# Router and experts of a three-part block: selection ahead of the list, and the residual kept in PSUM

## What is computed

```python
h2 = rms_norm_3(x, norm_ffn_w[l], NORM_EPS)
x = x + hierarchical_moe(h2, ...)
return rms_norm_3(x, final_norm_w, NORM_EPS)

def hierarchical_moe(h, w_gr, b_gr, w_er, b_er, w_gate, w_up, w_down):
    # each token picks one of 8 groups, and the best two of that group's 8 experts
    weights = g_gate[:, None] * jax.nn.softmax(top_v, axis=-1)
    ...
    def expert_block(args):
        xblk, e = args
        hid = jax.nn.silu(xblk @ w_gate[e]) * (xblk @ w_up[e])
        return hid @ w_down[e]
    ...
    out = jnp.zeros((n_tok, d)).at[buf_tok].add(yb * buf_w[:, None])
```

## Time and profile before

| | us |
|---|---|
| three runs: median (lowest to highest) | 2837.94 (2836.89 to 2840.13) |
| profiled execution, its own time | 2836.18 |
| its span in the trace | 2834.4 |
| TensorE busy (matmul), share of the span | 2708.1 (96%) |
| TensorE weight loads | 2280.6 (80%) |
| DVE busy | 1438.2 (51%) |
| ACT busy | 515.2 (18%) |
| DMA moved | 589.09 MB, 208 GB/s on average |

### The profile page before, as it was taken

How to read it: one execution, slowest core, us unless ns; L and a number is a source line. 1 busy time by engine, 2 the same in 40 slices (tenths; PEclk the granted TensorE clock), 3 DMA queues, 4 the chain that set the end, 5 groups by cost and what they waited for, 6 DMA issues and landing times. The chain is left out here.

```text
span 2834.4 us, 44443 instructions
## 1 busy us (share of the span) xinstructions
PE 2708.1 (96%) x18750; PEld 2280.6 (80%) x18750; DVE 1438.2 (51%) x2805; ACT 515.2 (18%) x1095; POOL 0.2 (0%) x4
## 2 busy tenths in 40 slices
PE   8999899999999999999999999999998898888887
PEld 8998799999988999888988998888896554444443
DVE  7768677687555775544345657365434111111112
ACT  1001410010043100223010012344302111111111
POOL 0000000000000000000000000000000000000000
PEclk9999999999999999999999999899999999999999
DMA  7644145355354453536544444555554899999997
GB/s 232 212 157 156 52 157 179 134 182 176 120 134 149 151 177 116 135 108 156 170 149 149 155 121 107 150 150 133 137 171 182 339 427 426 426 426 426 427 427 332
DMA packets 371212, 589.09 MB, mean 208 GB/s; under 512 B 17104, under 2 KB 328688, under 8 KB 348912
## 3 DMA queue, kind: packets, MB, share of 16 engines
q1 hardware_dynamic: 366256, 582.21, 58.4%
q10 hardware_dynamic: 4800, 4.63, 0.6%
HBM read 585.72 MB, written 1.08 MB: 207 GB/s over the span
## 5 line engine op out<-in xcount | busy, mean ns | idle before, releaser
L844 PE MATMUL bank<-hR,ring 128*128 128x128 f32 x2112 | 267.4, 277 | 3.9 <-DVE hR L426 3.9
L3498 DVE TENSOR_TENSOR wk<-bank,wk 128x256 f32<-128x256 f32 x43 | 26.1, 608 | 466.5 <-PE bank L3421 466.5
L844 PEld LDWEIGHTS bank<-hR,ring 128*128 128x128 f32 x2112 | 252.7, 194 | 4.9 <-DMA ring<-in_ffn_w_in 2.7
L3441 PE MATMUL bank<-ring,wk 128*64 128x512 f32 x688 | 157.1, 598 | 24.1 <-ACT wk L3458 24.1
L3421 PE MATMUL bank<-ring,wk 128*64 128x256 f32 x1344 | 153.0, 381 | 19.6 <-DMA ring<-in_w_expert_up 19.6
L3421 PEld LDWEIGHTS bank<-ring,wk 128*64 128x64 f32 x1344 | 94.3, 137 | 85.3 <-DMA ring<-in_w_expert_up 26.8
L1164 PE MATMUL bank<-big,ring 128*128 128x128 f32 x1320 | 159.6, 275 | 0.0
L1164 PEld LDWEIGHTS bank<-big,ring 128*128 128x128 f32 x1320 | 153.5, 192 | 0.1
L733 PE MATMUL bank<-hR,ring 128*128 128x256 f32 x704 | 152.3, 379 | 0.0
L733 PEld LDWEIGHTS bank<-hR,ring 128*128 128x128 f32 x704 | 133.8, 190 | 18.2
L2272 PE MATMUL bank<-big,ring 128*128 128x256 f32 x640 | 141.2, 379 | 1.5 <-ACT big L2844 1.0
(11 more groups left out here) (495 smaller groups left out, 4619.3 us busy)
## 6 DMA issues: line engine op xcount, KB each, us to landing
ring<-in_ffn_w_in SPq DMA_DIRECT2D x88, 1024.0 KB
ring<-in_w_expert_down SPq DMA_DIRECT2D x43, 2048.0 KB
ring<-in_w_in SPq DMA_DIRECT2D x96, 512.0 KB
ext<-in_w_expert_gate SPq DMA_DIRECT2D x22, 2048.0 KB, 25.6
big<-in_w_expert_up SPq DMA_DIRECT2D x22, 2048.0 KB, 25.8
ring<-in_w_expert_gate SPq DMA_DIRECT2D x21, 2048.0 KB
ring<-in_w_expert_up SPq DMA_DIRECT2D x21, 2048.0 KB
ring<-in_ffn_w_out SPq DMA_DIRECT2D x40, 1024.0 KB
```

What stands on the lines that cost most here:

```text
L844: last = nc.tensor.matmul(k.bank[:, 2 * (n % 4) + p // 4, (p % 4) * P:(p % 4 + 1) * P], a[:, c, m * P:(m + 1) * P], b[:, c, :], start=c == ...
L3441: last = nc.tensor.matmul(k.bank[m * SLOTS:(m + 1) * SLOTS, self.DOWN, :], ht[:, c * SLOTS:(c + 1) * SLOTS], self.piece(h, 2)[:, a:a + 512 ...
L3498: chain(v.tensor_tensor(by_row, up, gate, ALU.mult), self.hid_ready)
```

## The change

Four things are changed.

- The 16 transposes of the norm are now ordinary matmuls with the identity, the first of each bank with the start flag, so that later put-backs add to what they leave. The residual stays in banks 0 to 3: ACT's two copies, DVE's two clearings and TensorE's four clearing matmuls are gone, as are DVE's four last additions. The final squares and scalings read PSUM.
- DVE does the selection first, then the first tokens of the two guessed experts, which it copies to `first` at once, then the list, then the rest as before.
- TensorE gathers before it turns the list, and no longer after it.
- ACT copies the first block's window as soon as the sorted tokens are there, ahead of the destination rows. TensorE's wait for the destination rows and the later waits for the turned columns are moved into the first block; SP waits for the second count of `eid_ready` in place of the first.

The diff, cut to its core:

```diff
@@ TokenNorm.pe, act and dve
-                    last = nc.tensor.transpose(k.bank[:, 2 * t + b // 2, (c % 4) * P:(c % 4 + 1) * P],
-                                               k.xT[:, c, t * P:(t + 1) * P], k.c("ident"))
+                    last = nc.tensor.matmul(k.bank[:, 2 * t + b // 2, (c % 4) * P:(c % 4 + 1) * P], k.xT[:, c, t * P:(t + 1) * P],
+                                            k.c("ident"), start=c % 4 == 0, stop=True, skip_group_check=True)
...
-        for t in range(T):
-            last = nc.scalar.activation(k.x[:, t, :].rearrange("p (a n) -> p a n", a=2), k.bank[:, 2 * t:2 * t + 2, :], ACT.Copy)
-        last.then_inc(self.xn_ready, 1)
...
-        self.route.experts.empty(chain)
@@ FinalNorm.act and scale
-            act.wait_ge(self.experts.x_summed, n + 1)
-            nc.scalar.activation(k.wk[:, n * 512:(n + 1) * 512], self.quarter(k.x, n), ACT.Square, scale=1.0 / 32,
+            act.wait_ge(self.experts.put_done, self.experts.taken * 2 + (n + 1))
+            nc.scalar.activation(k.wk[:, n * 512:(n + 1) * 512], k.bank[:, n, :], ACT.Square, scale=1.0 / 32,
...
-        chain(nc.vector.scalar_tensor_tensor(x, x, k.ss[:, 10 + n // 2:11 + n // 2], k.r(self.row)[:, (n % 2) * 512:(n % 2 + 1) * 512],
+        chain(nc.vector.scalar_tensor_tensor(x, k.bank[:, n, :], k.ss[:, 10 + n // 2:11 + n // 2], k.r(self.row)[:, (n % 2) * 512:(n % 2 + 1) * 512],
@@ Route.pe and act
+        self.experts.gather(pe)
         pe.wait_ge(self.list_ready, 1)
         nc.tensor.transpose(k.bank[0:1, 4, P:2 * P], k.small[:, 0:1], k.c("ident")).then_inc(self.row_ready, 1)
-        self.experts.clear(pe)
-        self.experts.gather(pe)
...
+        act.wait_ge(self.eid_ready, 1)
+        act.wait_ge(self.experts.xs_taken, KC)
+        self.experts.take_window(act, slice(0, 1)).then_inc(self.experts.xg_ready, 1)
         act.wait_ge(self.row_ready, 3)
@@ Experts.pe and block
-        pe.wait_ge(self.route.rows_taken, 2)
-        pe.wait_ge(self.route.eid_ready, 2)
         self.block(pe, None, 1)
...
+            if i is None and j == 1:
+                pe.wait_ge(self.route.eid_ready, 3)
...
+        if i is None:
+            pe.wait_ge(self.route.rows_taken, 2)
@@ Experts.dve
-        for j in range(4):
-            dve.wait_ge(self.put_done, n * 2 + (j + 1))
-            quarter(j).then_inc(self.x_summed, 1)
-            if j == 2:
-                chain.sem = self.tail_chain
-                self.final.variance(dve, chain, 0)
+        chain.sem = self.tail_chain
+        self.final.variance(dve, chain, 0)
```

More of the change, by code:

```diff
@@ L3183, in dve @@
         cnt = k.bank[:, 7, 0:64]
-        nb, end, big = wk[:, 600:664], wk[:, 664:728], wk[:, 728:792]
         zero = wk[:, 928:992]
@@ L3188, in dve @@
         both, second = guess.at(guess.BOTH, 64), guess.at(guess.SECOND, 64)
[L3189 to L3200, removed]
         def every(row):
@@ L3217, in dve @@
         self.experts.select(chain)
+        of = wk[:, 464:528]
+        for n, oh in enumerate((guess.at(guess.FIRST, 64), second)):
+            tt(of, tokens, oh, ALU.mult)
+            chain(v.tensor_reduce(cols(14 + n, 1), of, AX, ALU.add))
+        chain(v.tensor_copy(k.first[0:1, 0:2], cols(14, 2)[0:1, :]), self.eid_ready)
+        nb, end, big = wk[:, 600:664], wk[:, 664:728], wk[:, 728:792]
+        chain(v.scalar_tensor_tensor(nb, counts, 0.5, guess.at(guess.NEITHER, 64), ALU.is_gt, ALU.mult))
+        for n in range(1, S // SLOTS):
+            chain(v.scalar_tensor_tensor(nb, counts, n * SLOTS + 0.5, nb, ALU.is_gt, ALU.add))
+        chain(v.tensor_tensor_scan(end, nb, zero, 0.0, ALU.add, ALU.add))
+        chain(v.tensor_scalar(big, end, k.c("row"), None, ALU.is_le))
+        chain(v.tensor_reduce(cols(1, 1), big, AX, ALU.add))
+        chain(v.tensor_scalar(cols(0, 1), cols(1, 1), float(NEXP - 1), None, ALU.min), self.list_ready)
+        chain(v.tensor_copy(k.rounds[0:1, 0:1], end[0:1, NEXP - 1:NEXP]))
+        chain(v.tensor_single_scalar(k.rounds[0:1, 1:2], k.rounds[0:1, 0:1], 1, ALU.logical_shift_right))
+        chain(v.tensor_single_scalar(k.rounds[0:1, 2:3], k.rounds[0:1, 1:2], 1, ALU.add))
+        dve.wait_ge(self.row_ready, 1)
+        chain(v.tensor_copy(k.eid[0:1, :], k.bank[0:1, 4, P:2 * P]), self.eid_ready)
         first = wk[:, 400:464]
@@ L3226, in dve @@
         tt(nb, end, nb, ALU.subtract)
-        of = wk[:, 464:528]
         chain(v.tensor_scalar(of, nb, k.c("row"), None, ALU.is_le))
@@ L3233, in dve @@
         chain(v.tensor_scalar(cols(2, 1), cols(2, 1), float(2 * S), None, ALU.min), self.list_ready)
[L3234 to L3237, removed]
         base, shift = wk[:, 200:264], wk[:, 320:384]
@@ L3276, in name_sems @@
         self.put_done = sem("put_done")
-        self.x_summed = sem("x_summed")
         self.tail_chain = sem("tail_chain")
@@ L3349, in sp @@
             self.load(sp, sp.value_load(k.gid[0:1, 1 - h:2 - h], min_val=0, max_val=NEXP - 1), None, h, guessed=True)
-        sp.wait_ge(self.route.eid_ready, 1)
+        sp.wait_ge(self.route.eid_ready, 2)
         self.load(sp, sp.value_load(k.eid[0:1, 0:1], min_val=0, max_val=NEXP - 1), None, 1)
@@ L3354, in sp @@
                 self.load(sp, sp.value_load(k.eid[0:1, bass.ds(i * 2 + (1 + h), 1)], min_val=0, max_val=NEXP - 1), i, h)
[L3356 to L3364, removed]
     def gather(self, pe):
@@ L3407, in pe @@
                 self.block(pe, i, h)
-        pe.wait_ge(self.y_taken, n * 2 + 2)
-        pe.wait_ge(self.gw_ready, n * 2 + 2)
+        pe.wait_ge(self.y_taken, n * 2 + 1)
+        pe.wait_ge(self.gw_ready, n * 2 + 1)
         self.put(pe, final=True)
@@ L3425, in block @@
         if i is not None:
-            pe.wait_ge(self.y_taken, self.at_block(i, 1, h, 1))
-            pe.wait_ge(self.gw_ready, self.at_block(i, 1, h, 1))
+            pe.wait_ge(self.y_taken, self.at_block(i, 1, h, 0))
+            pe.wait_ge(self.gw_ready, self.at_block(i, 1, h, 0))
             self.put(pe)
+        if i is None:
+            pe.wait_ge(self.route.rows_taken, 2)
         pe.wait_ge(self.sel_ready, 1)
@@ L3443, in block, with take_window @@
         last.then_inc(k.w_used, 1)
+    def take_window(self, act, index):
+        first = act.value_load(self.k.first[0:1, index], min_val=0, max_val=2 * S)
+        return self.k.nc.scalar.activation(self.window(), self.sorted_rows()[:, :, bass.ds(first, SLOTS)], ACT.Copy)
     def act(self, act, chain):
         k, nc = self.k, self.k.nc
-        def take_window(index):
-            first = act.value_load(k.first[0:1, index], min_val=0, max_val=2 * S)
-            return nc.scalar.activation(self.window(), self.sorted_rows()[:, :, bass.ds(first, SLOTS)], ACT.Copy)
         def block(i, h):
@@ L3455, in block @@
             act.wait_ge(k.w_used, self.freed(i, h, 2))
-            take_window(slice(1, 2) if i is None else bass.ds(i * 2 + (h + 2), 1)).then_inc(self.xg_ready, 1)
+            self.take_window(act, slice(1, 2) if i is None else bass.ds(i * 2 + (h + 2), 1)).then_inc(self.xg_ready, 1)
             act.wait_ge(self.ht_ready, self.at_block(i, 1, h, 1))
@@ L3460, in block @@
             nc.scalar.activation(self.w(self.Y, 512), k.bank[:, self.DOWN, :], ACT.Copy).then_inc(self.y_taken, 1)
-        act.wait_ge(self.route.eid_ready, 2)
-        take_window(slice(0, 1)).then_inc(self.xg_ready, 1)
+        act.wait_ge(self.route.eid_ready, 3)
         block(None, 1)
-        with act.Fori(0, self.rounds(act)) as i:
+        n = self.taken = self.rounds(act)
+        with act.Fori(0, n) as i:
             for h in range(2):
                 block(i, h)
-    def empty(self, chain):
-        chain(self.k.nc.vector.memset(self.w(self.Y, 512), 0.0), self.y_taken)
-        chain(self.k.nc.vector.memset(self.w(self.GW, S), 0.0), self.gw_ready)
     def select(self, chain):
@@ L3487, in dve @@
         part, gw, tm = k.pslot[:, 4:5], self.w(self.GW, S), self.w(self.TM, S)
-        def quarter(n):
-            x = k.x[:, n // 2, (n % 2) * 512:(n % 2 + 1) * 512]
-            return v.tensor_tensor(x, k.bank[:, n, :], x, ALU.add)
         def block(i, h):
```

## The result

| | before | changed |
|---|---|---|
| median of 20 runs, us | 2837.35 | 2843.86 |
| lowest to highest, us | 2834.27 to 2841.29 | 2841.96 to 2846.17 |
| span of the profiled execution, us | 2834.4 | 2843.0 |

The changed kernel is 6.5 us slower: the ratio is 1.0024, with a 95% interval of 1.0018 to 1.0030. The forecast was 2844.7 us, +6.8.

What follows compares the result with a forecast made beforehand. Bound: a full stream of expert-weight loads behind an idle stretch, its end moving with its start. Terms 1.8 − 2.9 + 2.1 + 6.3 − 0.5 = +6.8 on 2836.18, plus 1.76, give 2844.7 us; own range 2842.8 to 2847.

Steps and rivals of the forecast that it cites:

- Step 1: Norm on TensorE: 16 transposes become fp32 matmuls leaving two records each, 32 in 3.6 us instead of 1.75: +1.8 us.
- Step 2: DVE's selection begins where the list did, 2.89 us earlier, so the gather can start sooner: −2.9 us.
- Step 3: Without the clearing matmuls TensorE idles and the gather starts at half clock, taking 16.1 us: +2.1 us.
- Step 4: Between gather and first gate group: DVE waits for the list's turn, TensorE for DVE, destination rows at half clock: +6.3 us.
- Step 5: Residual copies, memsets, SP's wait for the list, Silu's table load and the loop's put-back wait: cost nothing.
- Step 6: Tail: ACT squares from PSUM 0.4 us earlier and the inverse skips the fourth addition, 0.1 us more: −0.5 us.
- DVE's idle time that ends with the turn: Sign in DVE's trace: 7 us of idle time, ending with the turn of the list.
- A: Rival: TensorE's clock doesn't fall, or is back at once; +2.5 us, 2840.4 us; chance 11%.
- B: Rival: the half clock lasts longer at the gather, the destination rows or both; +8 to +11, 2846 to 2849 us; 9%.
- C: Rival: as matmuls the norm's transposes cost four times as much; 2848.2 us; chance 2%.
- D: Rival: change works as meant, DVE's destinations ready near the gather's end, gate group 2.9 us behind it; 2835.4 us; 5%.
- E: Rival: the delay isn't passed on because the weight stream had slack; +0 with the tail's gain, 2837.4 us; 3%.

Runs made afterwards that it cites:

- E2: Changed kernel plus three 128x512 fp32 matmuls of constants on TensorE between the counts and the gather: 2840.17 us.
- E1: Changed kernel with DVE's copy of the turned list moved behind the destinations and weights: 2834.94 us, ratio 0.9993 to the kernel before.
- E3: Changed kernel plus seven matmuls of constants while TensorE waits for DVE, three ahead of the second turn and four behind it: 2842.35 us.
- E6: Kernel before with only the half of the change that keeps the residual in PSUM, order unchanged: 2841.74 us, ratio 1.0016.
- E4: Changed kernel with the 16 matmuls by the identity back in transpose mode, start flag only on the first of each bank: 2840.81 us.
- E7: Changed kernel with late copy of the list, three matmuls of constants ahead of the gather, and transpose mode: 2830.30 us, ratio 0.9973 to before.
- E9: The E7 kernel, with three matmuls of constants, run again in another set: 2830.41 us, ratio 0.9977 to the kernel before.

## Why the prediction held

The forecast was +6.8 us, 0.24%, and the medians give +6.5 and a ratio of 1.0024. By its steps, against the pair of profiles:

| step | forecast | profile |
|---|---|---|
| 1 transposes | +1.8 | +1.82 (3.57 − 1.75) |
| 2 selection first | −2.9 | −3.0 (end of step 1 to the gather) |
| 3 gather at half clock | +2.1 | +2.6 (16.63 − 13.99) |
| 4 wait for DVE, rows at half clock | +6.3 | +5.8 to the gate group, +0.4 in it |
| stream | 0 | +0.2 |
| 6 tail | −0.5 | −0.8 |
| sum | +6.8 | +7.1 |

The largest term and its cause were forecast rightly, but that the sum comes so near is in part luck. The gather cost 0.5 us more than forecast, the gate group 0.4 and the stream 0.2 that had been given as nothing, and against that the rows cost 0.45 less and the tail gained 0.3 more. Of the time in us, 2844.7 against 2843.86, 0.6 is the base: three runs of the kernel before gave 2837.94, twenty gave 2837.35.

*The bound.* Rightly read: a full stream behind an idle stretch. In all nine kernels of the first table the first load to the last up matmuls takes 603.8 to 604.7 us, whatever comes before.

*Step 1* was right to the hundredth, as the records of an fp32 matmul are twice a transpose's and no dearer each. The Trainium skill's factor of four (TensorE: Matmul & The Clock Gate, Terms) isn't borne out here; 3.57 against 1.75 us is two.

*Step 2* was right; the 0.1 us more is in the router's logits, 3.53 against 3.61 us.

*Step 3* had the right mechanism, shown by E2, and was mis-sized by 0.5 us. Six kernels went into the gather from an idle TensorE at half clock and took 15.8 to 17.0 us, 1.8 to 3.0 more than the 13.99; one value of 2.1 was taken for what is a spread. The Trainium skill (TensorE: Matmul & The Clock Gate, Part 1) has throttled as the default that activity releases; the trace agrees: 0.50 ahead of the clearing or the constants, 1.00 after.

*Step 4* was right in its size and shown by E1, and its inner split was off by little: the rows took 3.79 us instead of 4.24, and the gate group lost 0.4 us that had been given as nothing. E3 has both back with the clock up. The price in the forecast was made of two records of 0.265 us; in a run of 16 they take 0.237 each (3.79 us).

*Step 5* held. ACT's Silu table load (2218.47, 1.28 us) now comes behind the gate group and lies beside the up group, as was said; the turned list is copied by 2203.06, 15 us ahead of SP's first load. What was not seen is that the pause ahead of the first block is itself a risk (E6). It isn't in this change's path, since the rows and the wait stand there.

*Step 6* was mis-sized by 0.3 us. The squares from PSUM follow each other every 0.57 to 0.58 us, where from SBUF it was 0.61 and up, and the first comes 1.37 us after the start of the final put-back (2833.18) instead of 1.88 (2823.81 in the kernel before); so the root comes 3.09 us after it, not 3.74, and the scaling 3.60, not 4.33.

Of the signs given, one was wrong: DVE's idle time that ends with the turn was put at 7 us and is 13.15. It ran from the end of the list, near 2189.6, all through the rest of the gather. No term of the sum rested on it.

Of the rivals, A (the clock stays up) is out by the windows of the changed kernel and by E2 and E3. B (longer at half clock) came true in small, 0.5 us in the gather and 0.4 in the gate group, and not to its time of 2846 us and more. C is out by the 3.57 us of the changed kernel and by E4, D by the wait in the trace (the rows 7.94 us behind the gather) and by E1, which shows what it would have been (the gate group 2.9 us behind the gather), and E by E1 and the stream's length.

## What to carry to other kernels

When a step is moved ahead of another on one engine, look at what the other engines have written behind their wait for its old place: the change moved a turn of 0.3 us behind a gather of 14 us, and a whole chain of DVE work that had been hidden came to stand in line. Put copies of results that are needed late behind the work that is needed early (E1: 8.9 us for two lines). And matmuls that look like waste may be what raises the clock for the next ones; before removing them, see what TensorE does in their place (E2, and 1.8 us by the paths of the last table).

## What had not been expected of the hardware

In these kernels a pause of TensorE of 2 to 3 us did not always bring the clock down. A pause of 3.0 us left it at 1.00 in the kernel before and brought it down in E6; one of 2.0 us brought it down in one profile of three constants (E7), and one of 1.7 us did not in the other (E9). In E6 and E7 the fall shows behind the pause, when the next matmuls have begun, so they are the ones that pay: 1.7 us each time. In the changed kernel it came within the wait, 2.4 us behind the gather. So two executions of one kernel can differ by 1.7 us at such a place (gather 15.7 and 14.0 us with three constants). That it is the cause of the whole spread, 7 us between the lowest and highest of the kernel before, wasn't tested, and part of the spread arises earlier: in the thirteen profiles the first of the 16 transposes or matmuls, with the same code ahead of it, starts between 2159.70 and 2162.95 us.
